# Modulation rows in other tiles, and h's sums over four pairs ahead of seven-product pairs that begin at the seventh pair

## What is computed

```python
mod = (silu(c) @ ada_w + ada_b).reshape(B, 3, 3, D)          # 9216 values: 72 rows of 128
shift, scale, gate = mod[:, :, 0], mod[:, :, 1], mod[:, :, 2]
h = modulate(rms_norm_2(x, norm_g[0]), shift[:, 0], scale[:, 0])
x = x + 0.5 * gate[:, 0, None, :] * swiglu(h, ffn1_w_in, ffn1_w_out)
h = modulate(rms_norm_2(x, norm_g[1]), shift[:, 1], scale[:, 1])
x = x + gate[:, 1, None, :] * token_mixer(h, ...)             # pooling and a gated delta rule
h = modulate(rms_norm_2(x, norm_g[2]), shift[:, 2], scale[:, 2])
x = x + 0.5 * gate[:, 2, None, :] * swiglu(h, ffn2_w_in, ffn2_w_out)
return rms_norm_2(x, final_g)
# swiglu: gate, up = split(h @ w_in); (silu(gate) * up) @ w_out, hidden width 2816 = 22 x 128
```

## Time and profile before

| | us |
|---|---|
| time, median of 3 runs | 1809.32 |
| profiled execution, its own time | 1809.3 |
| its span | 1807.1 |
| PE busy in the span | 1782.5 (99%) |
| DVE busy | 1252.1 (69%) |
| ACT busy | 946.8 (52%) |
| POOL busy | 141.7 (8%) |
| PE in the chain that ended last | 92% of the span |

### The profile page before, as it was taken

How to read it: one execution, slowest core, us unless ns; L and a number is a source line. 1 busy time by engine, 2 the same in 40 slices (tenths; PEclk the granted TensorE clock), 3 DMA queues, 4 the chain that set the end, 5 groups by cost and what they waited for, 6 DMA issues and landing times.

```text
span 1807.1 us, 24794 instructions
## 1 busy us (share of the span) xinstructions
PE 1782.5 (99%) x9644; PEld 1472.2 (81%) x9644; DVE 1252.1 (69%) x2164; ACT 946.8 (52%) x1631; POOL 141.7 (8%) x161
## 2 busy tenths in 40 slices
PE   8999999999999999999999999999999999999998
PEld 6777777777888788998886877788888878999887
DVE  6777877776536778886559778745664779888533
ACT  5777777777423424565225766344432444656521
POOL 2100000000011110000100020100100200000010
PEclk9999999999999999999999999999999999999999
DMA  5432332332253572334534223310552423333331
GB/s 194 140 105 82 117 105 70 117 94 94 71 175 105 188 280 83 104 104 158 168 120 141 81 81 100 98 55 24 205 203 93 143 79 94 107 105 103 110 98 64
DMA packets 59780, 210.44 MB, mean 116 GB/s; under 512 B 6736, under 2 KB 9168, under 8 KB 59024
## 3 DMA queue, kind: packets, MB, share of 16 engines
q1 hardware_dynamic: 47248, 164.54, 28.1%
q0 software_dynamic: 12416, 44.31, 7.5%
HBM read 203.58 MB, written 5.25 MB: 116 GB/s over the span
## 4 chain that ended last, share of the span: by engine, by line
PE 92%; DVE 4%; ACT 2%; issue 1%; DMA 0%; SPq 0%; DVEq 0%; ACTq 0%
PE ps L1513 20%; PE ps L1516 19%; PE ps L1514 19%; PE ps L1548 5%; PE ps L1549 5%; PE ps L1551 5%; PE ps L1631 2%; PE ps L1655 2%; PE ps L1592 2%; PE ps L1593 2%; PE ps L1599 1%; PE ps L1684 1%; ACT wH L2353 1%; DVE wL L1844 1%; PE ps L1643 1%
## 5 line engine op out<-in xcount | busy, mean ns | idle before, releaser
L1844 DVE TENSOR_TENSOR wL<-wr,wH 128x1024 fp32r<-128x1024 f32 (+2 forms) x325 | 348.5, 1075 | 222.7 <-ACT wH L2353 222.0
L2353 ACT ACTIVATE wH<-wr 128x1024 fp32r<-128x1024 f32 (+2 forms) x325 | 301.4, 930 | 261.9 <-PE ps L1516 231.3
L1513 PE MATMUL ps<-hH,wH 128*128 128x512 f32 (+1 forms) x1000 | 403.3, 403 | 1.1 <-DVE hL L2011 1.0
L1516 PE MATMUL ps<-hH,wL 128*128 128x512 f32 (+1 forms) x1000 | 391.1, 391 | 1.0 <-DVE wL L1844 0.7
L1514 PE MATMUL ps<-hL,wH 128*128 128x512 f32 (+1 forms) x1000 | 389.6, 390 | 0.0
L1513 PEld LDWEIGHTS ps<-hH,wH 128*128 128x128 f32 (+1 forms) x1000 | 187.3, 187 | 53.4 <-issue 13.1
L1516 PEld LDWEIGHTS ps<-hH,wL 128*128 128x128 f32 (+1 forms) x1000 | 186.9, 187 | 44.9 <-DVE wL L1844 4.0
L1514 PEld LDWEIGHTS ps<-hL,wH 128*128 128x128 f32 (+1 forms) x1000 | 187.3, 187 | 38.2 <-issue 2.6
L1513 PE MATMUL ps<-gffn,wH 128*128 128x512 f32 (+1 forms) x422 | 160.8, 381 | 0.2 <-DVE xT L2125 0.2
L1514 PE MATMUL ps<-gffn,wH 128*128 128x512 f32 (+1 forms) x422 | 159.6, 378 | 0.0
L1516 PE MATMUL ps<-gffn,wL 128*128 128x512 f32 (+1 forms) x422 | 159.5, 378 | 0.0
(11 more groups left out here) (364 smaller groups left out, 3374.9 us busy)
## 6 DMA issues: line engine op xcount, KB each, us to landing
wr<-wst SPq DMA_DIRECT2D x280, 512.0 KB, 3.5
vffn<-wfd POOLq DMA_DIRECT2D x24, 512.0 KB, 5.7
fed<-wfd POOLq DMA_DIRECT2D x20, 512.0 KB, 3.8
xT<-wfd POOLq DMA_DIRECT2D x16, 512.0 KB, 4.3
wr<-wst SPq DMA_DIRECT2D x16, 384.0 KB, 3.0
affn<-wfd POOLq DMA_DIRECT2D x12, 512.0 KB, 4.7
xT<-xin SPq DMA_DIRECT2D x8, 256.0 KB, 7.1
xT<-xin SPq DMA_DIRECT2D x2, 1024.0 KB, 5.9
```

What stands on the lines that cost most here:

```text
L1513: e.matmul(o, hi, vh, start=k == 0, stop=False)
L1516: i = e.matmul(o, lo, vh, start=False, stop=k == t.nk - 1)
L1844: e.tensor_tensor(dst, x, hi.bitcast(F32), ALU.subtract).then_inc(s[name], 1)
L2353: e.activation(dst, x, ACT.Copy).then_inc(s[name], 1)
```

## The change

- The rows of mod are divided anew: 0 to 23 in the attention block (rows 16 to 23 in the z tiles of its output part, `out0`, at k = 5 of tiles h = 6 to 13), 24 to 47 in the `res` tiles of the first feed-forward (four to a tile, two buffers in `affn`), and 48 to 71 in the mixer's last part (one every 3.5 ticks instead of every 4, still two buffers, from the same tick). The gate and up tiles have none.
- `mod2` (shift and scale of the mixer, rows 24 to 39) stands in the fifth `res` tile, the first gate values are made in `mod`, and the two others in `mod3`. The mixer's raw high and low parts (`raw`) stand in the last three `res` tiles (RAW_STEPS) instead of one in each.
- SEVEN is (6, 6): the first feed-forward has 16 seven-pairs instead of 11, the second 16 instead of 17.
- T1 to T4 are made and rounded over pairs 2 to 5, a step every four k-steps, with `t_hi` and `t_lo` of T3 and T4 among them. `seven` loses its argument `sums`.
- The accumulator of the squares of the second norm (`square_sum(2)`) lies in another buffer.

```diff
@@ -117,11 +117,14 @@
 NFED = 72
-FED_FIRST = 16
-FED_LAST = 40
-FED_ENDS = (FED_FIRST, FED_LAST, 52, NFED)
-FED_BUFS = (3, 4, 1, 2)
-SEVEN = (11, 5)
+FED_FIRST = 24
+FED_MIX = 40
+FED_LAST = 48
+FED_ENDS = (FED_FIRST, FED_LAST, NFED)
+FED_BUFS = (3, 2, 2)
+FED_STEPS = [(0, 13), (0, 20)] + [(c, k) for c in range(1, 6) for k in (3, 9, 14, 20)] + [(6, 3), (6, 9)]
+RAW_STEPS = {(5, 5): (0, 1), (5, 11): (2,), (6, 5): (3, 4), (6, 11): (5,), (7, 5): (6,)}
+SEVEN = (6, 6)
@@ -612,7 +607,8 @@ out0
-            self.whole(Tile("z", src("l0_w_in", 6144 + 128 * h), self.pb01.take()[1], "h", ("zs", d["zs"]), n=0, d=d))
+            self.whole(Tile("z", src("l0_w_in", 6144 + 128 * h), self.pb01.take()[1], "h", ("zs", d["zs"]), n=0, d=d),
+                       (lambda: self.fed(10 + h)) if h < 14 else None)
@@ -678,14 +674,17 @@ ffn, res tiles
-                if n == 1 and (c, k) == (0, 14):
-                    add("fed_start", stage=2, after=("fu", 22), i=FED_LAST, n=FED_BUFS[2])
-                if n == 1 and 0 < c < 7 and k in (9, 20):
-                    self.fed(FED_LAST + 2 * (c - 1) + k // 20)
+                if n == 1 and (c, k) == (0, 5):
+                    add("fed_start", stage=1, after=("fu", 22), i=FED_FIRST, n=FED_BUFS[1])
+                if n == 1 and (c, k) in FED_STEPS:
+                    self.fed(FED_FIRST + FED_STEPS.index((c, k)))
+                if n == 1 and (c, k) == (4, 12):
+                    add("mod2")
+                if n == 1 and (c, k) in RAW_STEPS:
+                    for i in RAW_STEPS[c, k]:
+                        self.raw(2, i)
                 if k == 5 and c > 0:
                     square(c - 1)
-                    if n == 1:
-                        self.raw(2, c - 1)
@@ -722,29 +721,26 @@ sevens
         plan = [(t_sum, 1, 0), (t_sum, 1, 1), (t_sum, 1, 2), (t_sum, 2, 0), (t_sum, 2, 1), (t_lo, 1), (t_sum, 3, 0), (t_sum, 3, 1),
-                (t_sum, 3, 2), (t_lo, 2), (t_sum, 4, 0), (t_sum, 4, 1)]
-        turn = {3 * i: [one] for i, one in enumerate(plan)}
-        for i, at in ((1, 13), (2, 22)):
+                (t_sum, 3, 2), (t_lo, 2), (t_sum, 4, 0), (t_sum, 4, 1), (t_lo, 3)]
+        turn = {4 * i: [one] for i, one in enumerate(plan)}
+        turn[60] = [(t_lo, 4)]
+        for i, at in ((1, 17), (2, 30), (3, 42), (4, 56)):
             turn.setdefault(at, []).insert(0, (t_hi, i))
         self.whole(up(1))
-        if f == 0:
-            add("fed_start", stage=1, done=raw_done, i=FED_FIRST, n=FED_BUFS[1])
-        at = -16 * (begin - 5)
+        at = -16 * (begin - 6)
         for j in range(2, begin):
-            for i, t in enumerate((gate(j), up(j))):
-                for k in self.steps_of(t):
-                    if f == 0:
-                        self.fed_later(2 * (j - 2) + i, k)
+            for t in (gate(j), up(j)):
+                for _ in self.steps_of(t):
                     for fn, *a in turn.get(at, ()):
                         fn(*a)
                     at += 1
-                    if at == 36:
+                    if at == 52:
                         self.sums(f, begin)
-                    if at == 40:
+                    if at == 57:
                         add("sums", f=f, at=self.seven_units[f, begin], part=1)
@@ -1095,10 +1089,10 @@ mixer
-        add("fed_start", stage=3, after=("hn", 8), i=FED_ENDS[2], n=FED_BUFS[3])
-        for i in range(FED_ENDS[2], NFED):
-            at(B + 4 + 4 * (i - FED_ENDS[2]), self.fed, i)
-        at(B + 4 + 4 * (NFED - FED_ENDS[2]), lambda: add("mod3"))
+        add("fed_start", stage=2, after=("hn", 8), i=FED_LAST, n=FED_BUFS[2])
+        for i in range(FED_LAST, NFED):
+            at(B + 4 + 7 * (i - FED_LAST) // 2, self.fed, i)
+        at(B + 4 + 7 * (NFED - FED_LAST) // 2, lambda: add("mod3"))
...
```

More of the change, by code:

```diff
@@ L239, in fed @@
         self.add("fed", i=i, next=later if later < FED_ENDS[stage] else None, fed=self.sig("fed"))
[L241 to L247, removed]
     def raw(self, n, c):
@@ L746, in sevens @@
         for j in range(begin, 22):
-            late = self.seven(j, n, f, w_in, pb, late, (lambda: t_hi(3), lambda: t_lo(3), lambda: t_hi(4), lambda: t_lo(4)) if j == begin else None)
+            late = self.seven(j, n, f, w_in, pb, late)
         late()
@@ L753, in sums, with seven @@
         self.add("sums", f=f, at=d, part=0)
-    def seven(self, j, n, f, w_in, pb, late, sums):
+    def seven(self, j, n, f, w_in, pb, late):
         sig, add = self.sig, self.add
@@ L780, in seven @@
             add("splits", done=first + i + 1)
-            if sums is not None and i < 4:
-                sums[i]()
             if name == "p2" and j < 21:
@@ L1243, in model_kernel @@
             tH, tL = ({i: G.t[:, 512 * t0 + 2048 * t_at[i] + a:512 * t0 + 2048 * t_at[i] + a + 1024] for i in t_at} for a in (0, 1024))
-            if f == 0:
-                late_row, late_buf = V[:, 0:1024], [V[:, 1024 + 1024 * i:2048 + 1024 * i] for i in range(FED_BUFS[1])]
             A = Arena(F, f"affn{f}", 4992)
             if f == 0:
-                ff0_row, ff0_buf = A.t[:, 2560:3584], A.t[:, 3584:4608]
+                late_row, late_buf = A.t[:, 2560:3584], [A.t[:, 3584:4608], A.t[:, 1536:2560]]
             ff.append(dict(aH=aH, aL=aL, av=av, tH=tH, tL=tL, s_sum=[c5(V, c) for c in range(38, 42)],
@@ L1300, in fed_views @@
                 return late_buf[i % FED_BUFS[1]], late_row
-            if i < FED_ENDS[2]:
-                return ff0_buf, ff0_row
-            return mix_buf[i % FED_BUFS[3]], mix_row
+            return mix_buf[i % FED_BUFS[2]], mix_row
         s = {name: ctx.enter_context(nc.semaphore("s_" + name)) for name in plan.count}
@@ L1342, in square_sum @@
         def square_sum(n):
-            return {0: WT[:, 0:512], 1: acc1, 2: ff[0]["tmp"][0], 3: tq[0], 4: ff[1]["tmp"][0]}[n]
+            return {0: WT[:, 0:512], 1: acc1, 2: ff[0]["rs"], 3: tq[0], 4: ff[1]["tmp"][0]}[n]
         def norm_views(n):
@@ L2102, in _ @@
                     w.wait_ge(s["mod"], 1)
+                    own(e.tensor_scalar(gate[:, 0:8], mod[:, 16:24], 0.5, None, ALU.mult, ALU.bypass))
                     factors(range(1))
@@ L2111, in _ @@
                 elif what in ("mod2", "mod3"):
-                    a, b = (FED_FIRST, FED_LAST) if what == "mod2" else (FED_LAST, NFED)
+                    a, b = (FED_FIRST, FED_MIX) if what == "mod2" else (FED_MIX, NFED)
                     w.wait_ge(s["fed"], b)
@@ L2115, in _ @@
                     w.wait_ge(s["mod"], 2 if what == "mod2" else 3)
-                    for sub in (0,) if what == "mod2" else (1, 2):
+                    for sub in () if what == "mod2" else (1, 2):
                         own(e.tensor_scalar(gate[:, 8 * sub:8 * sub + 8], mod[:, 24 * sub + 16:24 * sub + 24], 0.5, None,
@@ L2747, in _ @@
                         w.wait_ge(s["nl"], d["nl"])
-                    elif d["stage"] == 1:
-                        w.wait_ge(s["slot"], d["done"])
                     else:
```

## The result

The changed kernel takes 1812.76 us (median of 18 runs, 1809.68 to 1816.27), the kernel before 1809.53 in the same sessions (18 runs, 1809.01 to 1810.14): a ratio of 1.0017, 95% interval 1.0011 to 1.0024. So it is 3.2 us slower, where 2.1 us faster was forecast and nothing above 1811.3 was in the range. Its runs also lie 6.6 us apart, those of before 1.1.

The account below looks back on a forecast made before the run. TensorE, busy 99% of the 1807.1 us span, was taken as the bound, so only its matmuls or holes count. 1809.3 - 3.2 (pairs) - 4.06 (seven-pair waits) + 5.2 (mixer stall) = 1807.2 us, range 1802.2 to 1811.3.

Parts of the forecast that it names:

- The products and the first seven-pairs: Both feed-forwards: four net pairs turned save 3.2 us, and waits inside the first seven-pairs go, 4.06 us.
- The third rival: First seven-pairs: sums, or DVE's wL in pairs 2 to 5, still late; the 4.06 us stay, 1811.3; chance 0.07.
- Rows in the z tiles and output tiles at no cost: Eight rows moved to z tiles, 24 instead of 12 in the first feed-forward's output tiles: counted as nothing.
- The step that decides: Mixer's z and gate tiles: 24 rows every 3.5 k-steps, two buffers; waiting rows hold wL, TensorE stands 5.2 us.
- Behind that point ... the turn can fall to 5.36: Mixer, behind the eleventh tile's wL: buffers turn faster, the fourteenth tile's wL is 5.0 late, nothing further lost.
- The second rival: Mixer: turn grows as row pairs issue behind a weight load; 1810.0 at 6.26, 1813.6 at 6.7; chance 0.12.
- its formula: Mixer stall taken as 8 turns less 42.06 us; from a turn of 6.16 it eats the whole gain.
- The rule on transfer times: Mixer's row transfers: about 2.0 us plus bytes over 436 GB/s, 3.2 us for 512 KB, so no wait.
- The first rival: The mixer's stretch keeps up with no stall: 1802.0, or 1803.5 with a small rest; chance 0.28.

Follow-up runs that it names:

- version with the mixer's part as before: The changed kernel with 20 mixer rows every 4 ticks, as before the change, and four rows more in the first feed-forward's output tiles: 1801.98 us, ratio 0.9959.
- The sums alone: The kernel before with only h's sums rounded over the four pairs ahead of the first seven-pair, SEVEN (11, 6): 1805.94 us, ratio 0.9981.
- the wait of known size: The version with the mixer's part as before, plus three unused 128x1024 operations on DVE behind the last row of mod: 1803.58 us.
- seven-pairs from the sixth pair: The version with the mixer's part as before, with SEVEN (5, 5) and all four sums rounded over three pairs: 1802.68 us, ratio 0.9962.
- the weights' bytes halved: The changed kernel with weight transfers in and behind the mixer's gate tiles carrying half their bytes, rows of mod whole: 1810.46 us, ratio 1.0007.
- mixer's rows alone: The kernel before with 24 rows every 3.5 ticks in the mixer's last part, two buffers, 8 instead of 12 in output tiles: 1820.11 us, ratio 1.0055.
- rows in pairs: The version with the mixer's part as before, its 20 rows issued two per 8 ticks, directly behind each other: 1812.63 us, ratio 1.0015.
- half of the rows' bytes: The changed kernel with row transfers in the mixer's last part, but the first two, carrying half their bytes: 1805.99 us, ratio 0.9981.

## Why the prediction was wrong

**The products and the first seven-pairs: right.** 5.32 us were forecast for the first feed-forward and 5.23 came; 1.94 for the second, and 2.0 came. All of it together, 7.26, is what the version with the mixer's part as before gained (7.4). The sums alone gave 3.4 (3.26). The third rival falls.

**Rows in the z tiles and output tiles at no cost: right**, with 28 rows in the output tiles too.

**The step that decides: the right place and mechanism, the wrong size.** A row waits, the wL behind it waits, TensorE stands at the third product: all that came. The sum had 5.2 us for it; it was 8.8 in the profile, and 10.8 by the medians with and without the part. The 2.0 us between these two stay open: the profiled run lies 2.0 below the median, and no slower run has a trace. Two sentences of the prediction failed. The first is "I take 5.2, since 5.91 is this very stretch's mean": the turn was taken as one number, the mean of a list in which rows alternate with a wL or a z product. The changed list has three rows between some wL, and two of them directly behind each other. Then POOL issues two transfers 1.15 to 1.8 us apart, and the second landed in 5.8 to 7.0 us instead of about 4. Up to the eighteenth row the mean came out near, 5.99 (from 1276.18 to 1324.14 in eight turns), but as one turn of 8.16 and seven of 5.69 on average; that it was so near is luck. The second sentence is "Behind that point ... the turn can fall to 5.36": there it was 7.70. With the stretch 5.2 us earlier than before, the eighteenth row was due at 1328.2 - 5.2 = 1323.0 and came at 1324.14. The eleventh tile's wL ended 6.4 us behind its time, not 5.2. The twentieth row came 7.70 later, while TensorE goes on 5.44 per tile, so the twelfth tile's wL ended at 1334.21, wanted at 1330.81 - 5.21 = 1325.6: 8.6 late. That is the loss of the profile. About 3 of these 8.6 us TensorE spent at half clock, the rest standing. An estimate from these turns: the two that follow a close issue are (8.16 - 5.69) + (7.70 - 5.69) = 4.5 us longer than the others, and with all turns at 5.69 the 18 rows ahead would still make the wL 4 us late. So by this estimate about half of the loss is the pairs, and half is the forecast's own reason, too many rows ahead of the wL.

The second rival had the cause in words ("pairs of rows now issue directly behind a weight load"), with 0.12. From the measured median, a stall of 10.8 by its formula is a turn of 6.6 in the mean, which it priced at 1813. The price is near what was measured, but not by its turn: the measured one was 5.99 and then 7.70 once. Rows read before would have hinted at it: where two transfers of a row's size were issued together, in the gate tiles, the median landing was 5.7, and the changed list showed where two rows would stand together. This row was kept for a bound of the rival and should have priced the pairs in the sum. (In the chances, 0.28 and a twentieth of 0.53 make 0.31, not 0.32.)

**The rule on transfer times.** The estimate of 3.2 us for 512 KB, from the Trainium skill (DMA: Bandwidth & Descriptors, "Anatomy of one DMA — SWDGE (gpsimd) path"), disagrees with the trace for a row that is alone as well: 3.6 us was the least in the changed kernel. The first rival, which it spoke for, fell for this list and came true as soon as a third buffer or another pace was there (1803.58 and 1802.50).

## What to carry to other kernels

A mean turn time of a buffer holds for the order of instructions in which it was measured. When a change puts two users of a two-buffer ring directly behind each other, price the second transfer from rows in which two stand as close (here mostly 5.8 to 7.0 us instead of about 4), count the users that stand ahead of each wL, and ask which instruction stands behind the waiting one. Here the same 24 rows by the same two buffers cost 10 us or nothing, by whether they came every 3.5 or every 4 k-steps.

## What the runs showed of the hardware

- A 512 KB transfer issued on POOL's queue under 1.9 us behind another landed in 5.8 to 7.0 us nine times in three profiles with two buffers, and in 4.9 once in each of three others (mixer's part as before, the wait of known size, seven-pairs from the sixth pair); with the weights' bytes halved it took 6.1 and 4.9. In the six profiles first named the other issues landed in 3.8 to 4.3 on average, single ones in up to 5.8. With four buffers, in the gate tiles of before, close ones took 4.6 to 6.9. With half the bytes close ones landed in 3.2 to 3.7.
- Waits of TensorE of 2.70, 2.52, 2.02 and 1.62 us were followed by 3 to 6 us at the 1.2 GHz level in four profiles (changed kernel, rows in pairs, half of the rows' bytes, half of the weights' bytes). Waits of 2.24, 2.81 and 2.72 us (mixer's rows alone) and of 2.92 (wait of known size) were not. So the length of the wait alone does not decide it; what does is open.
- The changed kernel's runs lie 6.6 us apart, those of before 1.1. Waiting on such a queue does not explain it alone: the mixer's rows alone waited longer, and those five runs lie 1.75 apart.
